# Two decoder layers on one core: the second output-projection panel by seven block products

## The reference, cut to what matters

```
def mixing_block(x, st, l, P, lb, pos0):
    proj = jnp.einsum('btd,de->bte', x, P['w_in'][l]).astype(jnp.float32)
    ...
    mixed = jnp.concatenate([ya, yb, yc, yd], axis=-1).astype(x.dtype)
    out = jnp.einsum('bte,ed->btd', mixed, P['w_out'][l])
    return out, (h1, buf1, c1, n1, m1, sr1, sh1)

def run_trunk(x, states, pos0, P, lb_all):
    for l in range(DEPTH):
        ...
        x = layer_norm(ALPHA * x + mix, P['ln_mix_g'][l], P['ln_mix_b'][l])
        if l % 2 == 0:
            ffn = swiglu(x, P['ffn_w1'][j], P['ffn_w3'][j], P['ffn_w2'][j])
        else:
            ffn = moe_swiglu(x, ...)
        x = layer_norm(ALPHA * x + ffn, P['ln_ffn_g'][l], P['ln_ffn_b'][l])
```

## Time and profile before

| | |
|---|---|
| median of 3 runs | 1014.73 us (1014.66 to 1015.68) |
| the profiled execution's own time | 1020.87 us |
| its span, from the first to the last instruction | 1019.1 us |
| mean granted TensorE clock in it | 0.995 of 2.4 GHz |
| PE busy | 994.4 us (98%) |
| DVE busy | 500.0 us (49%) |
| POOL busy | 79.3 us (8%) |

### The profile page before, as it was taken

How to read it: one execution, slowest core, us unless ns; L and a number is a source line. 1 busy time by engine, 2 the same in 40 slices (tenths; PEclk the granted TensorE clock), 3 DMA queues, 4 the chain that set the end, 5 groups by cost and what they waited for, 6 DMA issues and landing times.

```text
span 1019.1 us, 23916 instructions
## 1 busy us (share of the span) xinstructions
PE 994.4 (98%) x10773; PEld 826.0 (81%) x10773; DVE 500.0 (49%) x1023; ACT 192.3 (19%) x417; POOL 79.3 (8%) x102
## 2 busy tenths in 40 slices
PE   9999999999999999999999999999999999999995
PEld 6897877899999999988978878567887878878642
DVE  5888894764666654268778944420101201012034
ACT  1333332131111100133343322300000000000001
POOL 2010022500000000000000200320000020000020
PEclk9999999999999999999999999999999999999998
DMA  9327348214443155022242487799999999999961
GB/s 358 138 87 239 113 164 353 83 66 184 165 182 133 55 214 210 1 78 89 84 137 94 156 343 312 271 343 398 402 423 398 421 386 415 424 422 424 420 239 55
DMA packets 37323, 241.45 MB, mean 237 GB/s; under 512 B 5024, under 2 KB 8352, under 8 KB 17504
## 3 DMA queue, kind: packets, MB, share of 16 engines
q1 hardware_dynamic: 26896, 216.40, 53.8%
q0 software_dynamic: 6416, 19.52, 5.4%
q10 hardware_dynamic: 3904, 3.93, 1.3%
HBM read 228.60 MB, written 13.07 MB: 237 GB/s over the span
## 4 chain that ended last, share of the span: by engine, by line
PE 92%; DVE 4%; DMA 1%; issue 1%; ACT 1%; SPq 0%; DVEq 0%
PE ps L734 71%; PE ps L1281 14%; PE ps L1386 6%; DMA up_slots<-in_w_in 1%; PE ps L737 1%; DVE x L2132 1%; DVE overlay L2103 0%; DVE overlay L2102 0%; DVE overlay L2127 0%; DVE small L2301 0%; ACT up_slots L1710 0%; ACT overlay L1710 0%; DVE tables L2882 0%; DVE tables L2965 0%; DVE x L2095 0%
## 5 line engine op out<-in xcount | busy, mean ns | idle before, releaser
L734 PE MATMUL ps<-up_slots,mix_or_moe 128*32 128x352 f32 (+2 forms) x3248 | 240.6, 451 | 0.8 <-issue 0.8
L734 PEld LDWEIGHTS ps<-up_slots,mix_or_moe 128*32 128x32 f32 (+2 forms) x3248 | 151.1, 111 | 81.0 <-issue 13.1
L734 PE MATMUL ps<-x,up_slots 128*128 128x144 f32 (+3 forms) x816 | 152.2, 340 | 1.1 <-DMA up_slots<-in_w_in 0.9
L734 PEld LDWEIGHTS ps<-x,up_slots 128*128 128x128 f32 x816 | 123.8, 190 | 26.8 <-issue 7.6
L734 PE MATMUL ps<-overlay,tables 128*32 128x256 f32 (+5 forms) x2004 | 124.2, 374 | 1.1 <-DVE overlay L2103 0.8
L734 PEld LDWEIGHTS ps<-overlay,tables 128*32 128x32 f32 (+2 forms) x2004 | 108.7, 114 | 12.2 <-issue 1.8
L2921 DVE TENSOR_TENSOR mix_or_moe<-mix_or_moe,ps 128x352 f32<-128x352 f32 x24 | 11.2, 517 | 177.8 <-PE ps L734 177.8
L1281 PE MATMUL ps<-overlay,up_slots 128*128 128x144 f32 x704 | 91.2, 286 | 1.2 <-DVE overlay L2701 1.2
L1281 PEld LDWEIGHTS ps<-overlay,up_slots 128*128 128x128 f32 x704 | 88.3, 190 | 1.4 <-issue 1.4
L734 PE MATMUL ps<-up_slots 128*128 128x144 f32 (+2 forms) x768 | 87.1, 282 | 0.8 <-DVE up_slots L2382 0.5
L734 PE MATMUL ps<-overlay,up_slots 128*128 128x128 f32 (+3 forms) x560 | 86.0, 314 | 1.0 <-ACT overlay L1710 1.0
(11 more groups left out here) (350 smaller groups left out, 997.3 us busy)
## 6 DMA issues: line engine op xcount, KB each, us to landing
up_slots<-in_moe_w SPq DMA_DIRECT2D x64, 1408.0 KB, 20.6
overlay<-in_moe_w SPq DMA_DIRECT2D x21, 1536.0 KB, 22.0
up_slots<-in_ffn_w SPq DMA_DIRECT2D x30, 1024.0 KB, 6.9
up_slots<-in_w_in SPq DMA_DIRECT2D x27, 1024.0 KB, 5.0
up_slots<-in_w_out SPq DMA_DIRECT2D x8, 1024.0 KB, 6.3
overlay<-in_moe_w SPq DMA_DIRECT2D x7, 1024.0 KB, 22.7
mix_or_moe<-in_states POOLq DMA_DIRECT2D x6, 512.0 KB, 9.0
expert_tokens<-in_shape_tables POOLq DMA_DIRECT2D x8, 384.0 KB, 7.9
```

The costliest lines, as they stand in the source:

```text
L734: return pe.matmul(o, lhsT, rhs, start=start, stop=stop)
```

## The change

The second panel (u = 1) of both layers no longer takes 16 matmuls of 288 columns, but seven products of 4 matmuls of 144 columns each: the panel's weights are cut into four blocks (two halves of the input features by its two output tiles), the tokens into two halves, and seven products of sums of blocks give all four output blocks. That takes three sums of weight blocks and one in place (`s1`, `s2`, `a21`, `s4`, 128x512 each) and four of token blocks (`OTOK`, 128x576 each), all on DVE in front of `out_part(1)`, and eleven small steps on DVE behind the products in place of one residual step. Besides:

- Panel 0 goes to banks 4 and 5, so that PE waits for an earlier event (`ret_ac sd`) instead of the last eviction; the products use banks 2, 3 and 6.
- At the start of layer 1, tile 3 goes to bank 6 and is done in two token parts, as tile 2 is; its first part stands in front of `gates(second)`.
- `t1` for `up_p5(0)` is made in two parts, the first after 5 scaled tiles, and PE's matmuls wait for each part.

```diff
@@ seven-product steps, semaphore counts: helpers out_pe, out_dv, out_sum, out_tokens @@
+        OSUM = cut(OV, 8 * T, 3, KH, P)
+        OTOK = cut(OV, 16 * T, 4, KH, TH)
+        S1O, U2O, U3O = OV[:, 24 * T:24 * T + TH], OV[:, 24 * T + TH:25 * T], SM[:, 0:TH]
...
@@ PE, start of layer 1 @@
                     tile_out(3, lambda k: slot(1)[:, k, 0:P], KT, X, c=first)
+                    tile_out(6, lambda k: slot(1)[:, k, P:2 * P], KT, X, c=first)
                     gates(second)
                     proj_tile(0, second)
                     gate_rows()
                     proj_tile(1, second)
                     tile_out(3, lambda k: slot(1)[:, k, 0:P], KT, X, c=second).then_inc(S["in_ps"], 1)
-                for i in range(2 + l, 7):
+                    tile_out(6, lambda k: slot(1)[:, k, P:2 * P], KT, X, c=second).then_inc(S["in_ps"], 1)
+                for i in range(2 + 2 * l, 7):
                     proj_tile(i)
...
@@ PE, output projection @@
                 mix(l)
-                pe.wait_ge(S["in_ev"], N_IN * (l + 1))
+                pe.wait_ge(*mark("ret_ac", "sd", l))
...
-                            last = mm(PS[:, b, 0:T], slot(2)[:, k, b * P:b * P + P], mixed[:, k], k == 0, k == 3)
+                            last = mm(PS[:, 4 + b, 0:T], slot(2)[:, k, b * P:b * P + P], mixed[:, k], k == 0, k == 3)
...
-                for b in range(2):
-                    out_tile(1, b, slice(0, T), 2)
+                pe.wait_ge(*mark("mixed", "B", l))
+                out_product(2, w[:, 0:KH, 0:P], mixed[:, 0:KH, low], True, "p1")
+                pe.wait_ge(*out_sum(l, 0))
+                pe.wait_ge(*out_tokens(l, 0))
+                out_product(6, OSUM[:, 0], OTOK[:, 0], True, "p5")
+                pe.wait_ge(*out_sum(l, 1))
+                pe.wait_ge(*out_tokens(l, 1))
+                out_product(3, OSUM[:, 1], OTOK[:, 1], True, "p6")
+                pe.wait_ge(*out_dv(l, "s1"))
+                out_product(2, w[:, KH:KT, 0:P], mixed[:, KH:KT, low], False, "p2")
+                pe.wait_ge(*out_sum(l, 2))
+                pe.wait_ge(*out_tokens(l, 2))
+                pe.wait_ge(*out_dv(l, "u2"))
+                out_product(3, w[:, 0:KH, P:2 * P], OTOK[:, 2], False, "p7")
+                pe.wait_ge(*out_sum(l, 3))
+                pe.wait_ge(*out_dv(l, "s5"))
+                out_product(6, OSUM[:, 2], mixed[:, KH:KT, high], False, "p3")
+                pe.wait_ge(*out_tokens(l, 3))
+                pe.wait_ge(*out_dv(l, "u3"))
+                out_product(3, w[:, KH:KT, P:2 * P], OTOK[:, 3], False, None).then_inc(S["out_ps"], 1)
+                pe.wait_ge(S["in_ev"], N_IN * (l + 1))
                 for u in range(2, 4):
                     pe.wait_ge(full[2 + u], loaded["out", l, u])
-                    pe.wait_ge(out[0], out[1] + u - 1)
+                    if u == 3:
+                        pe.wait_ge(*out_dv(l, "low"))
...
@@ DVE @@
-                out_part(1, 0, everything, 0)
-                out_part(2, 1, everything, 2)
+                sig(tt(s1, a21, a22, AD), *out_sum(l, 0))
+                sig(tt(OTOK[:, 0], b12, b11, SU), *out_tokens(l, 0))
+                sig(tt(s2, s1, a11, SU), *out_sum(l, 1))
+                sig(tt(OTOK[:, 1], b22, OTOK[:, 0], SU), *out_tokens(l, 1))
+                tt(a21, a11, a21, SU).then_inc(S["sx_w"], 1)
+                tt(OTOK[:, 2], b22, b12, SU).then_inc(S["sx_t"], 1)
+                tt(s4, a12, s2, SU).then_inc(S["sx_w"], 1)
+                tt(OTOK[:, 3], b21, OTOK[:, 1], SU).then_inc(S["sx_t"], 1)
+                out_part(1, 0, everything, 4)
...
+                cp(S1O, PS[:, 2, 0:TH]).then_inc(S["sx_dv"], 1)
...
+                stt(low[:, TH:T], low[:, TH:T], ALPHA, PS[:, 6, 0:TH], M, AD).then_inc(S["sx_dv"], 1)
...
+                tt(U2O, S1O, PS[:, 3, 0:TH], AD).then_inc(S["sx_dv"], 1)
...
+                stt(top[:, 0:TH], top[:, 0:TH], ALPHA, PS[:, 2, 0:TH], M, AD)
...
+                tt(U3O, S1O, PS[:, 3, 0:TH], AD).then_inc(S["sx_dv"], 1)
...
+                link(stt(top[:, TH:T], top[:, TH:T], ALPHA, PS[:, 6, 0:TH], M, AD))
+                v.wait_ge(S["out_ps"], HALF_OUT * l + 2)
+                stt(low[:, 0:TH], low[:, 0:TH], ALPHA, PS[:, 3, 0:TH], M, AD).then_inc(S["sx_dv"], 1)
+                v.wait_ge(*out_dv(l, "low"))
+                tt(top[:, TH:T], top[:, TH:T], U2O, AD)
+                tt(low[:, TH:T], low[:, TH:T], U3O, AD)
+                tt(low[:, 0:TH], low[:, 0:TH], S1O, AD).then_inc(S["out_x"], 1)
+                tile_sum(1, everything, (S["out_x"], HALF_OUT * l + 2))
                 out_part(3, 2, first, 0)
```

More of the change, by code:

```diff
@@ L52 @@
 SEVEN_GROUPS = ((0, 2), (2, 5), (5, 7))
+OUT_PE, OUT_DV = "p1 p5 p6 p2 p7 p3".split(), "s1 s5 u2 u3 low".split()
 CAP, NG, GT = 96, 3, 32
@@ new lines, in _ @@
+                w = slot(3)
+                low, high = TOKEN_HALVES
+                pe.wait_ge(full[3], loaded["out", l, 1])
+                pe.wait_ge(*mark("mixed", "B", l))
[5 more added lines that the diff above has]
+                pe.wait_ge(*out_tokens(l, 1))
```

67 lines of the change are left out of this document (51 added, 16 removed).

## The result

The change makes the kernel slower: 1017.68 us median of 8 runs (1016.83 to 1018.56), against 1014.64 for the kernel before (8 runs, 1013.10 to 1015.68). The ratio is 1.0030, 95% interval 1.0021 to 1.0039, so +3.0 us. The time lies in the range given, but 1.7 us above the forecast of 1016.0, and what happened is not the forecast's case: it is the slower rival's, in which the clock falls in PE's new pause (1018.1). The range held because it was wide enough to take that rival in.

The account below looks back on a forecast made before the run. PE was taken to bound the kernel, busy for 994.4 of 1019.1 us. Layer 0 +3.0, layer 1 -1.72, tile 3 and `t1` 0 gave +1.3: 1022.2 profiled, 1016.0 as median, range 1012.7 to 1018.7.

Parts of the forecast that it names:

- the slower rival: Layer 0, before the mean: PE's 5.3 us pause lowers its clock, 2.1 us on top, +3.4, 1018.1; chance 0.18.
- The seven products: Panel 1, both layers: 28 matmuls of 144 columns take 6.85 us instead of 7.83, 0.98 less, if they never wait.
- Other banks: Start of panel 0, both layers: PE starts at 164.34 instead of 165.08 in layer 0, 0.74 us gained in each layer.
- The eight sums: DVE behind `mixed`, before the products: 5.80 us of weight and token sums, until 172.8, covered by DVE's former 6 us wait.
- The rival in which POOL catches panel 0's sum: Layer 0: DVE 0.35 us later, its sum waits for POOL's first addition; mean 3.8 late, +2.1, 1016.8; chance 0.08.
- One opening per addition in layer 0: Behind the products, DVE's two-SBUF-input additions get in once per POOL addition, 2.43 us apart; the mean comes 3.0 us later.
- the shared opening: Layer 0: the three closing additions run together between two POOL additions; mean only 0.5 later, total -1.2, 1013.5; chance 0.24.
- DVE held no more than before: Layer 0: extra additions cost only their own 0.31 us each, both layers gain 1.72; -3.4, 1011.3; chance 0.13.
- Layer 1: Output projection: without POOL contention, 1.72 us pass on to the mean, the norm and the experts.
- Tile 3 and `t1`: Layer 1's start and the feed-forward's `up_p5(0)`: splitting gains 0; up to 1.74 if DVE weren't last, and at most 0.2.
- The clock: PE behind layer 0's new pause: a fall priced at 2.1 us, kept as a rival outside the forecast's sum; chance 0.18.
- the prediction's own three signs of being wrong: L2769 and L2770 take 0.3 each, PE's clock drops behind 189, or the eight sums run past 173.

Follow-up runs that it names:

- The cut GpSimd additions: Changed kernel with GpSimd's feed-forward weight-block additions cut to 8 columns of each tile, leaving out part of the work; 1016.84 us against 1021.15 before, ratio 0.9953.
- the PSUM steps: Changed kernel with each panel 1 product added from PSUM straight to the residual; 1018.06 against 1021.15 us before, ratio 0.9968; repeated, 1011.58 against 1014.71, ratio 0.9966.
- ten idle matmuls: Changed kernel plus ten matmuls with unread results in layer 0, ahead of the mean; 1022.21 us, ratio to the kernel before 1.0005.
- third group: Runs of the PSUM steps again, and of that kernel with one closing addition back, `t1` whole, or banks 0 and 1; kernel before: 1014.71 us.
- one closing addition left: The kernel with the PSUM steps, with one addition of two SBUF inputs back behind the products in each layer; 1013.95 us, ratio to the kernel before 0.9986.

## Why the prediction was right, and where it was not

**The seven products** were to take 0.98 us less than dense in each layer, without a wait: panel 0's first matmul to panel 2's takes 14.62 us in both layers (179.19 − 164.57, 616.15 − 601.53), where 7.83 + 6.85 = 14.68 were counted.

**Other banks**: 0.74 us per layer were counted; in layer 1 the shift shrinks from 5.04 at the first level to 4.37 at panel 0, 0.67.

**The eight sums**: to end at 172.8; the last ended at 172.88, and the residual step and the sum behind it at 174.04, before POOL's first addition at 174.56. The rival in which POOL catches panel 0's sum did not occur.

**One opening per addition in layer 0**: the ends forecast were 181.65, 184.1, 186.5, 189.0, 191.6, 194.0 and 194.4; measured 181.82, 184.20, 186.57, 189.14, 191.66, 194.02 and 194.36. The mean was forecast 3.0 us later and came 2.96 later, the pause 5.3 and was 5.27. The prediction says that no row of before shows an addition behind another without a wait while POOL asks; L2103 behind L2102 in the earlier trace rows is just that, twice, as its own next sentences say. So the shared opening had less for it than its 0.24. The rule of the Trainium skill, page "SBUF — State Buffer", section "Who interferes with whom", by which the order of issue decides who is held, gave the same 3.0, and the rows agree with it (L2769 and L2770, issued with no wait behind another addition, took 2.46 and 2.45). The page has the hold for the whole instruction beside VectorE's two-port modes; these rows show it for additions with two inputs in SBUF. The cut GpSimd additions show the cause and the PSUM steps the remedy. Both faster rivals that hang on this fall: a shared opening, and DVE held no more than before.

**Layer 1** was forecast at −1.72; the shift falls from 5.04 to 3.37, −1.67.

**Tile 3 and `t1`** were forecast at nothing. A wait of 0.49 for a transfer, which the prediction didn't have, and one of 0.81 for the level stand where one wait of 1.7 was forecast, and the kernel without the parts is as fast. `t1` was costed at 0 to 0.2 and gives 0.17.

**The clock is the step that failed.** It is also one of the prediction's own three signs of being wrong ("if PE's clock drops behind 189"). The forecast's sum of +1.3 took PE's new pause of 5.3 us as idle time and no more, although the price of a fall had been worked out beside it, 2.1 us, and its own condition ("it decides only if PE really idles that long") was exactly what the forecast itself said would happen. The two were given 0.30 and 0.18 as if they excluded each other, when the pause of the first was the cause of the second. Measured: the clock fell in all three profiles with this pause (5.25 to 5.27 us; the changed kernel twice, and the one with tile 3 whole), and the mean clock of 7 of the 8 runs fits that; it cost 2.3 us from the mean to the variance, and 2.2 in the pair with and without ten idle matmuls. The price of 2.1 came close, but in part by luck: it was taken from the first matmuls of the earlier trace rows, and there the profile gives a granted clock of 1.00, so it is not shown that the clock made them slow. Here the Trainium skill, page "TensorE: Matmul & The Clock Gate", section "HAM oscillation — how this bites in real kernels", by which idle gaps between bursts throttle the array, pointed the right way, and the trace agrees: 0.50 from 193 to 199. With it the rows give 3.0 + 2.3 − 0.2 − 1.7 = +3.4 (the 0.2 is the shift that is lost between the variance, 5.28, and the first level, 5.04, most of it at `t1`), which is the shift of the experts' first matmul (649.90 behind 646.53) and the rival's +3.4; the medians give +3.0.

So the change is two good parts and a bad form: the banks and the products each shorten PE's work, and the way in which the products were put together, by three additions with both inputs in SBUF in a stretch where GpSimd runs its own, costs 4.9 us of wait (194.42 against 189.50 with the PSUM steps) and 2.3 of clock, of which the PSUM steps give back 0.7 as a wait behind the mean. With each product added from PSUM the change makes the kernel faster by 0.34% (0.9966, 0.9954 to 0.9978).

## What to carry to other kernels

Before adding VectorE work, count its instructions that read two SBUF operands in the stretches where GpSimd is busy with its own additions. In this kernel each cost the time of one GpSimd addition there (about 2.45 us), however short it is, while one that reads PSUM cost only itself (0.30 to 0.75). So fold the partial products from PSUM as they come, under the matmuls, and leave nothing for the end. When a forecast contains a new pause of the matrix engine of some microseconds, the clock's fall belongs in the forecast's own sum and is no rival to it, and a pause is best judged by what it does to the matmuls behind it. And cost the small edits against the openings too: 0.7 us earlier brought the mean forward by 1.7 where it caught one.

## What was not expected of the hardware

The clock also fell at pauses much shorter than 5.3 us: at one of 2.63 us (profiled once; 6 of 11 executions if the mean clock is a guide), at one of 2.31 us at the kernel's start, and at one of 1.73 us behind 4.04 us of idle matmuls (one execution in 11 by the mean clock, the profiled one). It is no rule: at a wait of 2.20 us at the start, in the third group's profile with the PSUM steps, it stayed up. It fell in none of the 11 executions with ten idle matmuls and no pause, by their mean clock (0.995 and 0.996). In the cases of 2.63 and 1.73 us it fell only while PE was already at work again, at about 192.8 (the pause ended at 191.63) and 195.7 (194.96): a matmul group that starts at full speed can still be slowed by the pause before it.

One start of the program differs from the next by up to 1.7 us at panel 0 (164.39 to 166.07 over kernels with the same work up to there, from the profiles), and VectorE and GpSimd don't move by the same: the first held addition takes 1.59 us (ten idle matmuls), 2.02 and 2.33 (eight) in kernels that don't differ ahead of it; where an opening is just caught or just missed, as with one closing addition left, executions of one kernel can differ by an opening and a clock's fall.
